# Two transformer blocks on one core: first-layer rotations by ScalarE's swapped copies alone, key rotations on GpSimd, the selection divided anew, the output in halves

## The reference, cut to what matters

```python
def dsa_attention(xn, w_in, w_o):
    q, k, v, qi, ki, wi = jnp.split(xn @ w_in, A_SPLITS, axis=-1)
    q, k, qi, ki = (apply_rope(t) for t in (q, k, qi, ki))   # 16, 4, 8, 1 heads of 64
    ...
    idx_logits = jnp.einsum('bqhd,bsd->bqhs', qi, ki)
    score = jnp.einsum('bqhs,bqh->bqs', relu(idx_logits), wi)
    _, sel = lax.top_k(where(admissible, score, -inf), 128)  # keys of each query
    ...  # softmax attention over the chosen keys

def apply_rope(x):        # x1, x2: the two halves (32 + 32) of a head
    return concatenate([x1 * cos - x2 * sin, x1 * sin + x2 * cos], -1)
```

## Time and profile before

| what | us |
|---|---|
| median of 3 runs (lowest, highest) | 2556.9 (2556.21, 2558.31) |
| the profiled execution's own time | 2555.74 |
| its span | 2554.4 |
| PE busy in it | 2517.0 (99%) |
| DVE, ACT, POOL busy | 1354.1, 1002.0, 1243.7 |
| rotations, index scores and selection until the first attention | about 30 to 145 |
| output behind the last matmul tile | about 2546 to 2554 |

### The profile page before, as it was taken

The page is one execution under the profiler, slowest core; times in us unless marked ns, Lnnn a source line. Parts: engine busy times, 40 slices in busy tenths (PEclk is TensorE's granted clock), DMA queues, the critical chain, the costliest instruction groups (busy, mean ns, idle before and its releaser), DMA issues.

```text
span 2554.4 us, 34162 instructions
## 1 busy us (share of the span) xinstructions
PE 2517.0 (99%) x13825; PEld 2068.2 (81%) x13825; DVE 1354.1 (53%) x2305; ACT 1002.0 (39%) x1711; POOL 1243.7 (49%) x609
## 2 busy tenths in 40 slices
PE   8999999999999999999999999999999999999999
PEld 6668888888777888888867888888888888888887
DVE  6984999943335699983885522124245223532121
ACT  6575423223357432233485533224233223432231
POOL 5784444444456454443686444444444344444442
PEclk9999999999999999999999999999999999999999
DMA  4111655622320465642401333323322222333321
GB/s 150 50 35 61 198 198 186 208 99 79 104 67 18 147 193 190 198 147 88 144 18 36 98 99 99 99 98 118 123 83 84 99 83 83 100 99 99 99 97 69
DMA packets 261184, 277.15 MB, mean 108 GB/s; under 512 B 7460, under 2 KB 249764, under 8 KB 260772
## 3 DMA queue, kind: packets, MB, share of 16 engines
q1 hardware_dynamic: 259428, 272.35, 32.9%
q10 hardware_dynamic: 1600, 2.62, 0.3%
HBM read 270.24 MB, written 2.10 MB: 107 GB/s over the span
## 4 chain that ended last, share of the span: by engine, by line
PE 90%; DVE 6%; ACT 2%; issue 1%; POOL 1%; DMA 0%; ACTq 0%; SPq 0%; DVEq 0%; POOLq 0%
PE bank L567 23%; PE bank L568 23%; PE bank L569 23%; PE bank L705 2%; PE bank L750 2%; PE bank L661 2%; PE bank L662 2%; PE bank L663 2%; PE bank L733 1%; DVE top L1763 1%; PE bank L586 1%; PE bank L526 1%; PE bank L982 1%; PE bank L587 1%; PE bank L588 1%
## 5 line engine op out<-in xcount | busy, mean ns | idle before, releaser
L1998 POOL TENSOR_TENSOR wlo<-raw,whi 128x1024 fp32r<-128x1024 f32 x406 | 993.8, 2468 | 1207.3 <-ACT whi L1038 1114.3
L1038 ACT ACTIVATE whi<-raw 128x1024 fp32r<-128x1024 f32 (+1 forms) x408 | 405.7, 1041 | 566.0 <-PE bank L569 488.7
L567 PE MATMUL bank<-Xhi,whi 128*128 128x512 f32 (+1 forms) x1560 | 613.1, 393 | 1.7 <-POOL wlo L1998 1.7
L568 PE MATMUL bank<-Xlo,whi 128*128 128x512 f32 (+1 forms) x1560 | 608.1, 390 | 0.0
L569 PE MATMUL bank<-Xhi,wlo 128*128 128x512 f32 (+1 forms) x1560 | 607.8, 390 | 0.0
L567 PE MATMUL bank<-Hhi,whi 128*128 128x512 f32 x976 | 379.9, 389 | 0.0
L569 PE MATMUL bank<-Hhi,wlo 128*128 128x512 f32 x976 | 379.7, 389 | 0.0
L568 PE MATMUL bank<-Hlo,whi 128*128 128x512 f32 x976 | 379.7, 389 | 0.0
L567 PEld LDWEIGHTS bank<-Xhi,whi 128*128 128x128 f32 (+1 forms) x1560 | 292.9, 188 | 69.9 <-issue 6.1
L569 PEld LDWEIGHTS bank<-Xhi,wlo 128*128 128x128 f32 (+1 forms) x1560 | 292.9, 188 | 62.0
L568 PEld LDWEIGHTS bank<-Xlo,whi 128*128 128x128 f32 (+1 forms) x1560 | 292.8, 188 | 60.4 <-issue 0.7
(11 more groups left out here) (318 smaller groups left out, 3388.6 us busy)
## 6 DMA issues: line engine op xcount, KB each, us to landing
ada<-in_ada_w SPq DMA_DIRECT2D x48, 1024.0 KB, 5.2
raw<-in_w_up SPq DMA_DIRECT2D x32, 1024.0 KB, 5.4
raw<-in_w_down SPq DMA_DIRECT2D x32, 1024.0 KB, 4.7
raw<-in_mlp_w_in SPq DMA_DIRECT2D x32, 1024.0 KB, 5.3
raw<-in_mlp_w_out SPq DMA_DIRECT2D x32, 1024.0 KB, 4.8
raw<-in_gmlp_w_in SPq DMA_DIRECT2D x24, 1024.0 KB, 5.0
raw<-in_gmlp_w_out SPq DMA_DIRECT2D x12, 1024.0 KB, 4.7
raw<-in_w_in_a SPq DMA_DIRECT2D x8, 1024.0 KB, 5.1
```

Source lines behind the costliest of these rows:

```text
L567: pe.matmul(b[0:rows, :], whi[s][:, c, j:j + rows], hi[:, c, :], start=(c == 0), stop=False)
L568: pe.matmul(b[0:rows, :], whi[s][:, c, j:j + rows], lo[:, c, :], start=False, stop=False)
L1038: act.activation(whi[u % 2][:, c0:c1, 0:k], src[:, c0:c1, 0:k], ACT_F.Copy).then_inc(hi_done, 1)
L1998: pool.tensor_tensor(low, src[:, c0:c1, 0:k], whi[u % 2][:, c0:c1, 0:k].bitcast(F32), ALU.subtract).then_inc(lo_done, 1)
```

## The change

- All fifteen rotations exchange halves by `swap_half` on ACT. `rotation` on PE, the constant perm and its load are gone. ACT's order in stage qa becomes: swap 5 before the first tile; before tiles 1 and 2 the key copies of r = 5 and 6; then hold, relus, and swap 6 + o behind tile o; swap 14 behind the first va tile.
- The key rotations (r = 5, 6) leave DVE. POOL makes sine product, cosine product and sum in held, and ACT copies each key head to both halves (`keys_out`, four copies of 64 rows each). On POOL rotation 6 goes behind the first index sums.
- DVE rotates 4, then 7 to 14, with new `cuts`: 18 pieces behind 4, and so on.
- The output: PE transposes chunks 0 to 3 of all four token blocks into banks 4 to 7 before the last tile, chunks 4 to 6 and then 7 behind it; ACT copies the first halves and half of the second ones, DVE the rest; eight stores of half the size.

```diff
-    BY_COPIES = range(7)
+    KEYS_A = {5: KA[0:2], 6: KA[2:4]}
     def rot_turned(r):
-        return (rot_swap, r + 1) if r in BY_COPIES else (rot_full, r - 6)
+        return rot_swap, r + 1
...
 # PE
-        def rotation(r):
...
-            pe.matmul(bank[4][:], perm[:], held[r % 3][:], start=True, stop=True).then_inc(rot_full, 1)
+        def turn_out(i, chunks):
+            for c in chunks:
+                pe_until.wait_ge(*freed(GEMM["m3d3"].tile + c))
+                m = pe.transpose(bank[4 + i][:, c % 4 * P:c % 4 * P + P], HT[:, c, i * P:(i + 1) * P], ident[:])
+            return m
...
+                if m == 3 and 8 * stage + o == 62:
+                    for i in range(NT):
+                        turn_out(i, range(4)).then_inc(o_full, 1)
...
         for i in range(NT):
+            pe_until.wait_ge(o_act, i + 1)
+            turn_out(i, (4, 5, 6))
+        for i in range(NT):
+            turn_out(i, (7,)).then_inc(o_full, 1)
 # ACT
+        def keys_out(r):
+            act_until.wait_ge(rot_sump, r - 4)
+            for i, k in enumerate(KEYS_A[r]):
+                for at in (0, 64):
+                    act.activation(k[at:at + 64, :], held[r % 3][64 * i:64 * i + 64, :], ACT_F.Copy).then_inc(key_copy, 1)
         def evac_qa(o):
             if o == 0:
                 swap_half(5)
-                swap_half(6)
-            if o == 5:
-                copy_keys(KA[0:2], 6)
-            if o == 6:
-                copy_keys(KA[2:4], 7)
+            if o in (1, 2):
+                keys_out(4 + o)
             hold("qa", 7)(o)
             for i, heads in INDEX_AFTER.get(o, ()):
                 relus(i, heads)
+            swap_half(6 + o)
...
+            if o == 0:
+                swap_half(14)      # behind the first va copy
 # DVE
-                src = tmp[2 + r % 2] if r in BY_COPIES else bank[4]
+                src = tmp[2 + r % 2]
-        cuts = (0, 12, 15, 21, 25, 32, 39, 44, 48, 52, 55, len(pieces))
-        for o in range(11):
-            rotation_a(4 + o)
+        cuts = (0, 18, 25, 31, 36, 41, 45, 49, 52, len(pieces))
+        for o, r in enumerate((4, 7, 8, 9, 10, 11, 12, 13, 14)):
+            rotation_a(r)
             select(cuts[o], cuts[o + 1])
 # POOL, in rotation(r)
+            if r in KEYS_A:
+                turned = tmp[2 + r % 2]
+                pool.tensor_tensor(turned[:], turned[:], rope[:, 1, :], ALU.mult).then_inc(rot_sinp, 1)
+                pool_until.wait_ge(rot_cos, r + 1)
+                pool_until.wait_ge(rot_sinp, r - 4)
+                pool.tensor_tensor(held[r % 3][:], held[r % 3][:], turned[:], ALU.add).then_inc(rot_sump, 1)
...
 # SP
         for i in range(NT):
             sp_until.wait_ge(o_act, i + 1)
-            sp_until.wait_ge(o_dve, i + 1)
-            sp.dma_start(out[0, i * P:(i + 1) * P, :], O[:, i, :]).then_inc(out_done, 16)
+            sp.dma_start(out[0, i * P:(i + 1) * P, 0:512], O[:, i, 0:512]).then_inc(out_done, 16)
+        for i in range(NT):
...
+            sp.dma_start(out[0, i * P:(i + 1) * P, 512:1024], O[:, i, 512:1024]).then_inc(out_done, 16)
```

More of the change, by code:

```diff
@@ L162, in body @@
     rcol, zcol, FG, GS = sb("rcol", [P, 2 * NT]), sb("zcol", [P, 2 * NT]), sb("FG", [P, KC]), sb("GS", [P, KC])
-    perm = sb("perm", [P, P])
     pick, warm, fold = sb("pick", [P, 19]), sb("warm", [P, 1]), sb("fold", [P, 32])
@@ L276, in body @@
     rot_swap = sem("rot_swap")
-    held_in, rot_full, rot_sin, rot_cos, rot_sum, rot_sump, key_copy, wi_full, wi_set = (
-        sem(n) for n in ("held_in", "rot_full", "rot_sin", "rot_cos", "rot_sum", "rot_sump", "key_copy", "wi_full", "wi_set"))
+    held_in, rot_sin, rot_cos, rot_sum, rot_sump, rot_sinp, key_copy, wi_full, wi_set = (
+        sem(n) for n in ("held_in", "rot_sin", "rot_cos", "rot_sum", "rot_sump", "rot_sinp", "key_copy", "wi_full", "wi_set"))
     swap_in = [sem(f"swap_in{i}") for i in range(3)]
@@ L402, in rot_adds, with rot_sines @@
     def rot_adds(r):
-        return (None, r - 6) if 7 <= r <= 14 else (r + 1 if r < 7 else r - 7, None)
-    BY_COPIES = range(7)
+        return (None, r - 4) if 5 <= r <= 14 else (r + 1 if r < 5 else r - 9, None)
+    KEYS_A = {5: KA[0:2], 6: KA[2:4]}
+    def rot_sines(r):
+        return r + 1 if r < 5 else r - 1
     def rot_turned(r):
-        return (rot_swap, r + 1) if r in BY_COPIES else (rot_full, r - 6)
+        return rot_swap, r + 1
     ROT_C = {15 + n: what for n, what in enumerate((("q", 0), ("q", 1), ("k", 0), ("q", 2), ("k", 1), ("q", 3), ("q", 4), ("q", 5), ("q", 6), ("q", 7)))}
@@ L698, in scores @@
                 if a == "a" and i == 0:
-                    pe_until.wait_ge(rot_sump, c + 1)
+                    pe_until.wait_ge(rot_sump, c + 3)
                 for e in range(2):
@@ L818, in after_qa @@
         def after_qa(o):
-            if o:
-                rotation(6 + o)
             for i, heads in INDEX_AFTER.get(o, ()):
@@ L824, in tensor_program @@
         fm("qa", X, chunk_a, after_qa)
-        tm("va", chunk_a, lambda o: rotation(14) if o == 0 else None)
+        tm("va", chunk_a)
         pe_until.wait_ge(idx_relu, 24)
-        pe_until.wait_ge(rot_sum, 7)
-        pe_until.wait_ge(rot_sin, 15)
-        pe_until.wait_ge(key_copy, 4)
+        pe_until.wait_ge(rot_sin, rot_sines(14))
+        pe_until.wait_ge(key_copy, 8)
         attention("a", "va",
@@ L939, in after_vc @@
             if o == 2:
-                pe_until.wait_ge(rot_sum, 17)
-                pe_until.wait_ge(key_copy, 8)
+                pe_until.wait_ge(rot_sum, 15)
+                pe_until.wait_ge(key_copy, 12)
                 pe_until.wait_ge(qn_set, 1)
@@ L1130, in evacuate @@
                 wait_tile(g)
-                if r >= 3:
+                if r - 3 in KEYS_A:
+                    act_until.wait_ge(key_copy, 4 * (r - 7))
+                elif r >= 3:
                     by_dve, by_pool = rot_adds(r - 3)
@@ L1354, in swap @@
             if r >= 18:
-                act_until.wait_ge(rot_sin, r - 2)
+                act_until.wait_ge(rot_sin, rot_sines(r - 3))
             for h in range(2):
@@ L1372, in evac_qc @@
             if o in (5, 6):
-                copy_keys(KCC[2 * o - 10:2 * o - 8], ROT_C_AT["k", o - 5] - 7)
+                copy_keys(KCC[2 * o - 10:2 * o - 8], ROT_C_AT["k", o - 5] - 9)
             if o in (2, 3):
@@ L1380, in evac_qc @@
             if o >= 3:
-                act_until.wait_ge(rot_sum, ROT_C_AT["q", o - 3] - 7)
+                act_until.wait_ge(rot_sum, ROT_C_AT["q", o - 3] - 9)
             act.activation(held[o % 3][:], bank[g % 4][:], ACT_F.Copy, scale=VEC["qg"])
@@ L1437, in scalar_program @@
         for i in range(NT):
-            act_until.wait_ge(o_full, 2 * i + 1)
-            act.activation(O[:, i, 0:512], bank[(LAST_TILE + 2 * i) % 4][:], ACT_F.Copy).then_inc(o_act, 1)
+            act_until.wait_ge(o_full, i + 1)
+            act.activation(O[:, i, 0:512], bank[4 + i][:], ACT_F.Copy).then_inc(o_act, 1)
+        for i in (0, 2):
+            act_until.wait_ge(o_full, NT + i + 1)
+            act.activation(O[:, i, 512:1024], bank[4 + i][:], ACT_F.Copy).then_inc(o_act, 1)
     def vector_program(dve):
@@ L1597, in rotation_sum @@
             dve_until.wait_ge(rot_cos, r + 1)
-            dve_until.wait_ge(rot_sin, r + 1)
+            dve_until.wait_ge(rot_sin, rot_sines(r))
             dve.scalar_tensor_tensor(dst, rotated(r)[:], 1.0, tmp[2 + r % 2][:], ALU.mult, ALU.add).then_inc(rot_sum, 1)
@@ L1786, in rotation_a @@
                 rotation_sum(n, QI[:, (0, 1, 1, 2, 3)[n], :])
-            elif n < 7:
-                rotation_keys(n, KA[2 * (n - 5):2 * (n - 5) + 2])
         dve_until.wait_ge(vec_full, 2)
@@ L1837, in vector_program @@
         dve.tensor_tensor(PBB[7][:].rearrange("p (i c h) -> p i c h", c=8, h=16), *copies, ALU.subtract).then_inc(lf_dve, 1)
-        dve_until.wait_ge(const_in, 48)
+        dve_until.wait_ge(const_in, 32)
         dve.tensor_copy(PICK[:], pick[:, 0:16]).then_inc(ck_dve, 1)
@@ L1982, in vector_program @@
         mlp(3, mod(1, 5))
-        for i in range(NT):
-            dve_until.wait_ge(o_full, 2 * i + 2)
-            dve.tensor_copy(O[:, i, 512:1024], bank[(LAST_TILE + 2 * i + 1) % 4][:]).then_inc(o_dve, 1)
+        for i in (1, 3):
+            dve_until.wait_ge(o_full, NT + i + 1)
+            dve.tensor_copy(O[:, i, 512:1024], bank[4 + i][:]).then_inc(o_dve, 1)
     def gpsimd_program(pool):
@@ L2079, in after_qa @@
                 rotation(5, rope_a)
-            rotation(6 + o, rope_a)
+            else:
+                rotation(6 + o, rope_a)
             for i, heads in INDEX_AFTER.get(o, ()):
                 index_sums(i, heads)
+            if o == 0:
+                rotation(6, rope_a)
         units("qa", after_qa)
@@ L2156, in sync_program @@
             sp.dma_start(dst, src).then_inc(vec_in, 16)
-        for dst, name in ((head_mean, "head_mean"), (perm, "perm_half"), (pick, "pick")):
```

(16 more changed lines are left out.)

8 lines of the change are left out of this document (1 added, 7 removed).

## The result

The changed kernel takes 2566.55 us (median of 5 runs, 2566.36 to 2567.33), the kernel before 2556.76 beside it: ratio 1.0041, 95% interval 1.0031 to 1.0052, so 9.8 us slower where +4.6 was forecast, and half a microsecond above the range. The profiled execution has a span of 2565.2, 10.8 over that of before; the medians differ by 1.0 less because the profiled execution of before lay 1.0 under its median.

What follows compares the result with a forecast made beforehand. PE is busy 99% of the span, but DVE bounds 61 to 146 us. Stage +4.6, clock +0.5 and output -0.5 give +4.6 on 2555.74, 2560.3; the median lies 1.2 higher: 2561.5 us, range 2555.5 to 2566.

Steps and rivals of the forecast that it cites:

- What bounds: From 61 to 146 us DVE's chain, narrowly ahead of PE, sets the time; the question is when ACT's copies arrive.
- The waits: In the selection, DVE waits 5.6 us for copy 7 and 5.1 for copy 8, ending 2.3 late despite 6.7 less work.
- Sines: DVE's sine products 9 to 12, reading SBUF beside POOL, take 0.9 us more each, 3.6 together.
- ACT's copies 10 to 14 come early, and DVE leads: Late selection: after sine 9 DVE has the same pieces and sines as before and sets the pace.
- Last mask: End of the selection: POOL's weight parts end before DVE's last mask, which gets shorter by 1.3 us (0 to 1.6).
- Stage: Up to the first attention: 2.3 + 3.6 - 1.3 = +4.6 us, DVE's first attention instruction at 149 to 150.
- PE's clock: Entry into the first attention: PE, nearly idle from 141 to 149, may start at the lower clock, +0.5 us (0 to +2).
- Output: Kernel's end: half the transposes, copies and bytes hide under the last tile, -0.5 us (-1.2 to +1).
- What follows (first attention) starts later by the whole sum: Behind the selection: the +4.6 us carries through, since PE is full there and nothing has slack to give it back.
- PE's removed perm products and waits are worth nothing: Up to the first attention: PE's sixteen perm matmuls taken away gain no time in the stage.
- Rival 3: First layer: sines 9 to 12 meet POOL's long weight parts (6.8), PE's clock +2: +9.3, 2566.2 us; chance 0.15.

Runs made afterwards that it cites:

- sums_first: The changed kernel with DVE's selection pieces divided otherwise and POOL's index sums put ahead of its rotations: 2555.99 us.
- copies_in_bank: The changed kernel with ACT's swapped copies 7 to 14 written to a PSUM bank, where DVE's sine products read them: 2564.95 us.
- tail_only: The kernel before with only the output by halves, its rotations untouched: 2555.86 us, ratio 0.9996.
- before_36_fewer: The kernel before with 18 first-MLP matmuls left out, so 36 PE instructions fewer ahead of the third attention: 2561.64 us.
- cos_after_sum: The changed kernel with POOL's last cosine product ahead of the third attention made to wait for DVE's sum of rotation 23: 2564.52 us.
- sums_and_cos: The changed kernel with the edits of sums_first and cos_after_sum together: 2552.08 us, ratio 0.9986.

## Why the prediction was half right

- **What bounds.** Right: DVE's in-order list up to the first attention, with ACT's copies as what it waits for. sums_first shows the cause: without those waits the loss is gone.
- **The waits.** 5.6 and 5.1 forecast, 6.53 and 5.93 measured. The copies ended at 83.60 and 96.33 (83.72 and 96.14 forecast), but this execution began 1.0 us earlier, so DVE stood there sooner. The key groups took 2.59 and 2.57, not 2.30 (L1152), and only ACT's lack of any gap made that count.
- **Sines.** 3.6 forecast; 0.69, 1.11, 1.53 and 2.60 are 3.2 over four at 0.68. copies_in_bank shows the source as the cause. These numbers, 0.68 or 0.69 from the bank and up to 2.60 from SBUF, agree with the rule of the Trainium skill's page "SBUF — State Buffer", section "Who interferes with whom".
- **"ACT's copies 10 to 14 come early, and DVE leads".** Not quite: sine 12 waited 0.57, since copy 12 stands behind tile qa6 in ACT's list, and POOL split qa6's weights only at 113.85 to 118.54.
- **Last mask.** 1.96 to 0.43, -1.5 for -1.3.
- **Stage.** +4.6 forecast with the attention at 149 to 150; it came at 150.43, +5.4, or 6.5 from the same start. It adds up: 13.3 of waits and 3.2 of longer sines come in; 6.7 of work, the 1.6 of waiting for POOL's sums and 1.5 of the last mask go; that is 6.7.
- **PE's clock.** +0.5 forecast. From DVE's first attention instruction to 250 us the changed kernel loses 1.9 on before, with this in the profile (columns as in the earlier trace rows):

```profile
141.00:149.00 8.00, 0.93 (x8) 0.55 (x8) 7.66 (x17) 0.01 (x1) 5.88 (x3) 0.66 0.08 20
150.00:154.00 4.00, 3.23 (x10) 2.43 (x12) 3.23 (x17) 2.80 (x11) 1.50 (x3) 0.52 0.36 127
```

  But tail_only and before_36_fewer, with before's rotations, lose 1.5 and 1.4 there on the same trace of before, and copies_in_bank and cos_after_sum, with the changed ones, only 1.0. The trace of before was a lucky one: granted 1.00 from 150 to 155, where tail_only and before_36_fewer have 0.66 and 0.73. What of the 1.9 is the change's stays open.
- **Output.** -0.5 forecast, -0.56 in the profile, -0.75 (not told from zero) in tail_only. The first halves' transposes and copies went under the last tile, as worked out:

```profile
2551.83 1.91 PE L831 MATMUL bank<-ident,HT 128*128 128x128 f32 x16
...
2552.46 2.06 ACT L1439 ACTIVATE O<-bank 128x512 f32<-128x512 f32 x4 [14.69 <-PE bank L831]
```

- **The step that failed** is "What follows (first attention) starts later by the whole sum", taken as a rigid shift of all that follows, with "PE's removed perm products and waits are worth nothing": behind the entry into the first attention the sum has no term but the output. Measured against it in the profile: the stage 5.4 for 4.6, the clock 1.9 (open) for 0.5, the output -0.56 for -0.5, the third attention 4.0 for nothing. The removed work was worth nothing; the number of instructions was not. 36 instructions fewer moved an instruction packet behind the last swap of the third attention, the swap landed 0.8 us sooner, POOL's product got ahead of DVE's sum, and 4.0 us were lost in code that nobody touched. Rival 3 came within half a microsecond of the time by luck: its long sines (6.8) were 3.2, and it has no third attention either. Its 2566.2 also lay above the stated range, whose upper end was to take it in.

## What to carry to other kernels

Before an engine's work is moved to another, write out the receiving engine's calendar and then reorder the waiting lists by it: here the same change with the lists of DVE and POOL reordered is 10.6 us faster. Where it hangs on half a microsecond which of two engines starts first, an edit far off may turn the order, as 36 instructions did here from 1130 us away; such an order belongs under a semaphore (one wait gave 3.6 us back by the profile, 3.9 in the medians of sums_first and sums_and_cos). And compare the traces at landmarks all the way to the end, also where the code is the same.

## What the hardware showed that was not expected

- Queue 8 carries TensorE's instructions: 109 packets of 16 KB for 27,650 recorded matmuls and weight loads, so some 254 a packet, or 256 from packet to packet with the waits counted. The packet at the third attention starts when PE has started 14,243 to 14,253 instructions, in every one of the 13 traces, so adding or dropping 36 of them ahead of it moved it. A packet that starts 1 us after a swap's issue (it takes 0.9 to 1.6 us) ends that swap's data at 3.0 to 3.7 us; one that starts behind the data leaves it at 2.26 or 2.27, in every trace here.
- A transfer that landed 0.8 us sooner made the third attention 4.0 us longer.
- 18 matmuls less in a stretch where PE is shown full (15 of 15 us) gained nothing: 3.0 us of their 4.1 went to a wait for DVE, busy 14.4 of 15 us, and 1.6 to a stretch at the lower clock behind that wait.
